# A transformer layer pair on one core: key and query turns placed between the chunks of the compressing products, and the products behind them inside the pair loop

## The chip, the cores and the metric

The kernel runs on one core of a Trainium2 chip. The core has five engines that run side by side and are tied together by semaphores: TensorE (PE in the profile; PEld are its weight loads), VectorE (DVE), ScalarE (ACT), GpSimd (POOL) and SyncE (SP, which issues DMAs). PE writes only to PSUM, whose banks are shared out by hand here; DVE and ACT copy from there to SBUF. The metric is the device time of one execution in microseconds (us), as the median of several runs.

## What is computed

Two blocks on 512 tokens of width 1024 follow each other; only a part of the second matters here, an attention over compressed keys and values, over blocks and over a window. Cut to that part:

```python
def compress(kv_raw, pos, w1, w2):
    blocks = kv_raw[:, idx] + pos            # 31 blocks of 32 tokens, step 16, 2 groups of 64 columns
    return jax.nn.gelu(blocks @ w1) @ w2     # hidden width 256, out 64

q  = rms_norm_2(q, q_norm_g)
kc = rms_norm_2(compress(kcr, ...), k_cmp_norm_g)
vc = compress(vcr, ...)
# for each block of queries
s = einsum('bqghd,bngd->bghqn', q, kc) * scale;  p = masked_softmax(s);  o_cmp = p @ vc
s = einsum(q_rope, k_slc_rope);                  o_slc = masked_softmax(s) @ v_slc
s = einsum(q_rope, k_win_rope);                  o_win = masked_softmax(s) @ v_win
out = g0 * o_cmp + g1 * o_slc + g2 * o_win

y = gelu(s5(u));  ssm = y * sigmoid(y @ glu_w + glu_b) * silu(z_s)
x + gate * (concat(out * silu(z_a), ssm) @ w_out)
```

## The kernel before

Every engine has its own program in one file, in the order in which it is written; no scheduler moves anything. A wait stands in front of the instruction that needs it, and all that is queued behind it on that engine waits too. On ACT and DVE the helper `step` also waits for each instruction's own end.

The stretch in question begins when PE has finished the gate products of the state-space half (`glu`, four banks). Then, on PE:

- *Turns.* `turn(name, blocks, ready)` transposes four 128x128 blocks into one of the two turn banks `U`; `turn_bank()` waits until the bank's last user but one has been copied out. DVE copies with `take_turn`. There are four turns of roped keys (`k2`), four of normed queries (`q`, they go to tiles 14 to 17) and four of roped queries (`qr`, tiles 18 to 21).
- *Compressing products.* `compress("k")` and `compress("v")` sum 32 products 62x256 each, in four chunks of eight; each chunk's weights are a DMA of 1 MB into one of four ring slots. SP asks for a chunk when the chunk four places before it has been used (`used`). ACT drains each result through Gelu into `HROW` ("hidden k", "hidden v").
- *What follows.* The hidden rows are turned, DVE copies them to `HIDK` and `HIDV`, PE makes the second products with `w2_k` and `w2_v` into the three `gemm` banks `G`, and ACT copies the results to `KCRAW` ("have kc") and, in four pieces, to `VB` ("have vcmp").

DVE meanwhile finishes the gate of the state-space half ("zs gated"), copies the key turns, rotates the queries in four parts (`rope`), makes the four GLU products ("ssm out") and copies the query turns.

Then comes the pair loop: 32 steps, each for two heads of one block of 128 queries; the first 16 are of the block attention, the next 16 of the window attention, with 1, 2, 3 and 4 blocks of keys in turn, four steps each. In step p PE makes the scores of pair p (`pair_scores`, into one of two double banks `PAIR`), the sums of pair p-2 (`pair_sums`) and the turns of the probabilities of pair p-1 (`pair_turns`). DVE takes the maximum of pair p, copies the turns of pair p-1, and at odd p closes a group of four heads (`pair_finish`); ACT makes the exponents. The compressed attention is spread over the same steps: `compressed(p)` on DVE (norm of the compressed keys in steps 0 and 1, their turned copy in step 2, softmax in steps `CMP_AT` to `CMP_AT` + 6 with `CMP_AT` = 4), `compressed_scores` on PE at step 4 (32 rows, 64 wide), `compressed_turn` at 11 and 12, `compressed_sums` at 14, 15, 16 and 18. At step 7 DVE also makes the product with the attention gate (2048 wide). The double banks swap their roles at `CMP_AT`, since the compressed scores take one.

In the profile L822 are the turns, L1145 the compressing products, L685 the other products by `product`, L1224 and L1227 pair scores, L1236 pair turns, L1250 pair sums, L1186 the compressed scores; on DVE L1766 is `take_turn`, L1808 `tt`, L1814 `stt`, L2522 the pair maxima; on ACT L1311 is `drain`, L1664 the copies to `VB`, L1674 the exponents.

## Time and profile before

| | us |
|---|---|
| median of three runs (lowest, highest) | 1598.39 (1596.98, 1600.68) |
| the profiled execution, its own time | 1598.52 |
| its span, first to last instruction | 1596.7 |
| PE busy | 1441.1 (90%) |
| DVE busy | 948.9 (59%) |
| ACT busy | 513.2 (32%) |
| mean granted clock of TensorE | 0.943 of full |

Busy shares are means over stages with very different limits. A timeline row gives the start, the length of a run of like instructions, the line, the tile written and the tiles read, the count, and in brackets the idle time before it with what ended it. The granted clock is 1.00 at 2.4 GHz and 0.50 at 1.2 GHz. A 32-bit matmul shows as two rows, a turn of a block as one.

### The profile page before, as it was taken

What the parts mean: (1) busy time and instruction counts of PE and PEld (TensorE: products, weight loads), DVE (VectorE), ACT (ScalarE), POOL (GpSimd) and SP (SyncE); (2) the same over time, 40 slices, a digit from 0 to 9 for tenths busy, and PEclk for the clock granted to TensorE, in tenths of its full rate; (3) what the DMA queues carried; (4) which work ended last, traced back from release to release, by engine and by line L of the source; (5) the groups of instructions that cost most, each with busy time, mean ns of one, the idle gap of its engine ahead of it and who ended that gap; (6) DMA issues with size and microseconds to landing.
All of it is one profiled execution on the core that took longest, in us unless ns stands there. A gap on an engine that the chain in (4) does not pass through costs nothing.

```text
span 1596.7 us, 18675 instructions
## 1 busy us (share of the span) xinstructions
PE 1441.1 (90%) x7046; PEld 1098.3 (69%) x7046; DVE 948.9 (59%) x1596; ACT 513.2 (32%) x829; POOL 52.7 (3%) x43
## 2 busy tenths in 40 slices
PE   5998888896999776998999999999798999988998
PEld 4758788784566654886788888888477854566653
DVE  6259767666266768774545555533593748758830
ACT  5346332231232565133432433533213222123300
POOL 0000000000000440000000000000000002000000
PEclk9999999997989879999999999999898999979999
DMA  5212111122222121452144434132321222410001
GB/s 226 71 53 80 66 40 53 60 91 67 89 88 73 47 74 54 143 182 97 66 145 181 150 144 160 55 109 94 111 82 37 80 78 81 166 71 1 1 1 53
DMA packets 39881, 140.50 MB, mean 88 GB/s; under 512 B 13040, under 2 KB 17520, under 8 KB 27248
## 3 DMA queue, kind: packets, MB, share of 16 engines
q1 hardware_dynamic: 34608, 130.53, 23.5%
q10 hardware_dynamic: 5184, 8.78, 1.5%
q8 instruction: 56, 0.92, 0.2%
q14 instruction: 33, 0.27, 0.1%
HBM read 128.42 MB, written 8.39 MB: 86 GB/s over the span
## 4 chain that ended last, share of the span: by engine, by line
PE 53%; DVE 6%; ACT 1%; issue 1%; ACTq 0%; DVEq 0%
PE turn L700 22%; PE score L685 6%; PE score L700 5%; PE sum L685 4%; PE turn L685 3%; PE sum L700 2%; PE sum L1250 2%; PE sum L1145 1%; PE score L1224 1%; PE turn L1236 1%; DVE heads L1808 1%; DVE work L1808 1%; DVE tiles L1814 1%; PE score L1289 1%; DVE probs L1766 0%
## 5 line engine op out<-in xcount | busy, mean ns | idle before, releaser
L1808 DVE TENSOR_TENSOR ring_r<-ring,heads_r 128x1024 fp32r<-128x1024 f32 (+3 forms) x153 | 176.3, 1152 | 223.1 <-ACT heads_r L1342 187.6
L1342 ACT ACTIVATE heads_r<-ring 128x1024 fp32r<-128x1024 f32 (+3 forms) x153 | 153.4, 1002 | 240.6 <-DMA ring<-wstream 129.5
L700 PE MATMUL score<-h_sb_r,heads_r 128*128 128x512 f32 x376 | 151.6, 403 | 0.0
L700 PE MATMUL turn<-tiles_r,heads_r 128*128 128x512 f32 x336 | 132.1, 393 | 0.0
L700 PE MATMUL turn<-h_sb_r,heads_r 128*128 128x512 f32 x304 | 119.7, 394 | 8.1 <-DVE ring_r L1808 8.1
L700 PE MATMUL turn<-wide_r,heads_r 128*128 128x512 f32 x312 | 121.9, 391 | 0.0
L700 PE MATMUL turn<-wide_r,ring_r 128*128 128x512 f32 x312 | 121.6, 390 | 0.0
L700 PE MATMUL score<-x_sb_r,heads_r 128*128 128x512 f32 x256 | 110.2, 430 | 8.9 <-DVE ring_r L1808 6.5
L700 PE MATMUL score<-x_sb_r,ring_r 128*128 128x512 f32 x256 | 103.8, 406 | 0.0
L700 PEld LDWEIGHTS score<-h_sb_r,heads_r 128*128 128x128 f32 x376 | 73.9, 197 | 13.7 <-issue 0.2
L700 PEld LDWEIGHTS turn<-tiles_r,heads_r 128*128 128x128 f32 x336 | 64.1, 191 | 13.2
L700 PEld LDWEIGHTS turn<-h_sb_r,heads_r 128*128 128x128 f32 x304 | 57.9, 190 | 20.5 <-issue 8.4
L700 PE MATMUL sum<-h_sb_r,heads_r 128*128 128x512 f32 x168 | 67.7, 403 | 0.0
L700 PEld LDWEIGHTS score<-x_sb_r,heads_r 128*128 128x128 f32 x256 | 51.2, 200 | 23.6 <-issue 10.6
L700 PEld LDWEIGHTS turn<-wide_r,ring_r 128*128 128x128 f32 x312 | 58.8, 189 | 12.3
L700 PEld LDWEIGHTS turn<-wide_r,heads_r 128*128 128x128 f32 x312 | 58.8, 188 | 12.3
L700 PEld LDWEIGHTS score<-x_sb_r,ring_r 128*128 128x128 f32 x256 | 50.8, 198 | 11.5
L1674 ACT ACTIVATE tiles<-score,stat 128x128 f32<-128x128 f32 (+3 forms) x64 | 33.7, 527 | 71.9 <-issue 65.3
L685 PE MATMUL score<-h_sb,ring 128*128 128x512 f32 x128 | 55.8, 592 | 0.0
L2571 POOL TENSOR_TENSOR stat<-stat,cst 128x4 f32<-128x4 f32 (+4 forms) x7 | 16.1, 2295 | 1187.2 <-DVE stat L1811 810.5
L1311 ACT ACTIVATE tiles<-score 128x512 f32<-128x512 f32 x39 | 24.3, 622 | 93.2 <-PE score L685 41.9
L700 PE MATMUL turn<-h_sb_r,ring_r 128*128 128x512 f32 x128 | 50.5, 395 | 0.0
(399 smaller groups left out, 2965.6 us busy)
## 6 DMA issues: line engine op xcount, KB each, us to landing
ring<-wstream SPq DMA_DIRECT2D x95, 1024.0 KB, 4.9
ring<-wstream SPq DMA_DIRECT2D x16, 704.0 KB, 4.3
ring<-gated SPq DMA_DIRECT2D x6, 1024.0 KB, 7.1
gated<-tiles ACTq DMA_DIRECT2D x15, 256.0 KB, 2.0
gated<-probs ACTq DMA_DIRECT2D x9, 256.0 KB, 2.0
x_sb<-xT SPq DMA_DIRECT2D x4, 512.0 KB, 5.7
x_sb<-xT ACTq DMA_DIRECT2D x1, 2048.0 KB, 8.0
outT<-x_sb SPq DMA_DIRECT2D x1, 2048.0 KB, 6.3
```

What stands on the lines that cost most here:

```text
L685: mm = pe.matmul(out, l, r, start=(i == 0), stop=(i == len(pairs) - 1))
L700: return pe.matmul(out, a, w, **k) if moving else pe.matmul(out, w, a, **k)
L1145: mm = pe.matmul(b[0:2 * NCMP, 0:256], CB[kv][:, 8 * i + l, :], w[:, l, :], start=(i + l == 0), stop=(8 * i + l == 31))
L1224: pe.matmul(PAIR_OF(p)[:, e * T:e * T + cols], TL[r, 18 + j, n * P:(n + 1) * P], KT2[r, 2 * a_ + j // 2, 0:cols], start=True, stop=False)
L1236: mm = pe.transpose(b[:, j * P:(j + 1) * P], PROB(i)[:, j * P:(j + 1) * P], ident)
L1250: mm = pe.matmul(OUT[g][:, h % 4 * P:h % 4 * P + P], PROBT(i)[:, j * P:(j + 1) * P], R2[:, j, at_v:at_v + P], start=(j == 0), stop=(j == n))
L1289: mm = pe.matmul(S[e], w[:, e, k, :], TL[:, 6 + k, :], start=False, stop=(k == 3))
L1311: step(act.activation(out, b, func, bias=bias, scale=scale), name, gemm_done)
L1342: step(act.activation(head_piece(p), chunk(name)[:, c:c + cols], ACT.Identity), f"head {p}")
L1674: step(act.activation(PROB(i)[:, 0:cols], PAIR_OF(p)[:, i % 2 * T:i % 2 * T + cols], ACT.Exp, bias=stat[:, 8 + i % 4:9 + i % 4], scale=1.0 ...
L1808: step(dve.tensor_tensor(out, a, b, op), name)
L2571: step(pool.tensor_tensor(v, v, half.broadcast_to([P, n]), ALU.pow), f"rstd {name}")
```

## The change

On PE, `compress` becomes a generator that stops after each chunk. Two key chunks come first, then two key turns, a chunk, two key turns, a chunk, two query turns, a value chunk and so on; the last value chunk comes after the hidden turn of the key. The hidden turn of the value moves into step 0 of the pair loop, the second product of the key into step 1 and that of the value into step 2; both go to turn banks. DVE copies their results in place of ACT. What followed of the compressed attention moves by one step (`CMP_AT` 4 to 5, turns at 12 and 13, sums at 15, 16, 17, 19). DVE's copies and rotations are put into the matching order. Cut to its core:

```diff
...
-    CMP_AT = 4
+    CMP_AT = 5
...
                         mm = pe.matmul(b[0:2 * NCMP, 0:256], CB[kv][:, 8 * i + l, :], w[:, l, :], start=(i + l == 0), stop=(8 * i + l == 31))
                     mm.then_inc(cmp_used if i < 3 else gemm_full, 1)
                     up(cmp_used if i < 3 else gemm_full, f"used cmp_{kv}{i}")
+                    yield
+
+            def hidden_turn(kv):
+
+                turn(f"hidden {kv}", [(HROW(kv)[0:2 * NCMP, k * P:(k + 1) * P], 2 * NCMP, 64 * k) for k in range(2)],
+                     (gemm_done, at(f"hidden {kv}")))
 
 
...
+            compressing = itertools.chain(compress("k"), compress("v"))
+            run(compressing, 2)
             for i in range(4):
                 turn(f"k2 {i}", [(K2(i)[:, n, :], P, n * P) for n in range(NT)], (dve_step, at("k roped")))
-            compress("k")
+                if i % 2:
+                    run(compressing, 1)
             for j in range(4):
                 turn(f"q {j}", [(R2[:, n, j * P:(j + 1) * P], P, n * P) for n in range(NT)], (dve_step, at("q normed")))
-            compress("v")
+                if j % 2:
+                    run(compressing, 1)
             for j in range(4):
                 turn(f"qr {j}", [(QR[:, n, j * P:(j + 1) * P], P, n * P) for n in range(NT)], (dve_step, at("q roped")))
-            for kv in "kv":
-                turn(f"hidden {kv}", [(HROW(kv)[0:2 * NCMP, k * P:(k + 1) * P], 2 * NCMP, 64 * k) for k in range(2)],
-                     (gemm_done, at(f"hidden {kv}")))
-            for kv in "kv":
-                b = gemm_bank()
+                if j == 1:
+                    run(compressing, 1)
+            hidden_turn("k")
+            run(compressing)
+
+            def hidden_out(kv):
+
+                b = turn_bank()
                 pe.wait_ge(turn_done, at(f"hidden T {kv}"))
...
-                mm.then_inc(gemm_full, 1)
-                up(gemm_full)
+                mm.then_inc(turn_full, 1)
+                up(turn_full)
 
...
                 if p == 0:
-                    pe.wait_ge(turn_done, at("hidden T v"))
+                    pe.wait_ge(turn_done, at("qrT 3"))
                 elif p == 1:
-                    pe.wait_ge(gemm_done, at("have vcmp"))
+                    pe.wait_ge(gemm_done, at("hidden v"))
                 elif p == CMP_AT + 1:
                     pe.wait_ge(dve_step, at("cmp masked"))
...
                 if 1 <= p <= 32:
                     for i in (2 * p - 2, 2 * p - 1):
                         pair_turns(i)
-                if p == 2:
+                if p == 0:
+                    hidden_turn("v")
+                if p in (1, 2):
+                    hidden_out("kv"[p - 1])
+                if p == 3:
                     turn("kc", [(KC2[0:NCMP, g, :], NCMP, 32 * g) for g in range(2)], (dve_step, at("kc normed")))
-                if p in (11, 12):
-                    compressed_turn(p - 11)
-                if p in (14, 15, 16, 18):
-                    compressed_sums((14, 15, 16, 18).index(p))
+                if p in (12, 13):
+                    compressed_turn(p - 12)
+                if p in (15, 16, 17, 19):
+                    compressed_sums((15, 16, 17, 19).index(p))
...
-            drain(KCRAW[0:NCMP, :], "have kc", cols=P, rows_=NCMP)
-            k = drained[0]
-            drained[0] += 1
-            act.wait_ge(gemm_full, k + 1)
-            for z in range(4):
-                r = slice(32 * z, 32 * z + 32)
-                step(act.activation(VB[r, :].rearrange("p (g d) -> p g d", g=2)[:, :, 64 * z:64 * z + 64],
-                                    G[k % 3][r, 0:P].rearrange("p (g d) -> p g d", g=2), ACT.Identity),
-                     "have vcmp" if z == 3 else None, gemm_done if z == 3 else act_step)
...
-            for i in range(4):
-                take_turn("kT 3" if i == 3 else None, KT2[:, i, :])
...
                 rope(qv[:, :, 0:32], qv[:, :, 32:64], cb, sb_, ta, tb, qd[:, :, 0:32], qd[:, :, 32:64], name="q roped" if n == NT - 1 else None)
+                if n < 2:
+                    for i in range(2):
+                        take_turn(None, KT2[:, 2 * n + i, :])
+            for j in range(4):
+                take_turn(None, TL[:, 14 + j, :])
             for j in range(4):
                 dve.wait_ge(gemm_done, at(f"glu {j}"))
                 stt(TL[:, 2 + j, :].rearrange("p (m a) -> p a m", a=STEP), H[:, 4 + j, :].rearrange("p (a m) -> p a m", a=STEP), 1.0,
                     TL[:, 10 + j, :].rearrange("p (a m) -> p a m", a=STEP), ALU.add, ALU.mult, "ssm out" if j == 3 else None)
-            for j in range(4):
-                take_turn(None, TL[:, 14 + j, :])
+                if j % 2:
+                    for i in (j - 1, j):
+                        take_turn(f"qrT {i}", TL[:, 18 + i, :])
             for cleared in (VB, part(rows, 2176, 512), part(rows, 2944, 128)):
                 step(dve.memset(cleared, 0.0), "cleared" if cleared is VB else None)
-            for j in range(4):
-                take_turn(None, TL[:, 18 + j, :])
             take_turn("hidden T k", HIDK[:, :, 0:2 * NCMP], cols=P, view=lambda v: v.rearrange("p (k t) -> p k t", k=2)[:, :, 0:2 * NCMP])
-            m = turned[0]
-            turned[0] += 1
-            dve.wait_ge(turn_full, m + 1)
-            for g in range(2):
-                src = U[m % 2][:, 0:P].rearrange("p (k t) -> p k t", k=2)[:, :, g * NCMP:(g + 1) * NCMP]
-                step(dve.tensor_copy(HIDV[:, :, g, :].rearrange("p k (r n) -> p k r n", r=4)[:, :, :, 0:NCMP],
-                                     src.unsqueeze(2).broadcast_to([P, 2, 4, NCMP])),
-                     "hidden T v" if g else None, turn_done if g else dve_step)
...
                 if p == 0:
-                    dve.wait_ge(gemm_done, at("have vcmp"))
+                    m = turned[0]
+                    turned[0] += 1
+                    dve.wait_ge(turn_full, m + 1)
+                    for g in range(2):
+                        src = U[m % 2][:, 0:P].rearrange("p (k t) -> p k t", k=2)[:, :, g * NCMP:(g + 1) * NCMP]
+                        step(dve.tensor_copy(HIDV[:, :, g, :].rearrange("p k (r n) -> p k r n", r=4)[:, :, :, 0:NCMP],
+                                             src.unsqueeze(2).broadcast_to([P, 2, 4, NCMP])),
+                             "hidden T v" if g else None, turn_done if g else dve_step)
+                if p == 1:
+                    take_turn(None, KCRAW[0:NCMP, :], cols=P, rows_=NCMP)
...
                     ts(stat[:, 32:34], stat[:, 32:34], 1.0 / 64, EPS, ALU.mult, ALU.add, name="mean kc")
-                if p == 1:
+                if p == 2:
+                    m = turned[0]
+                    turned[0] += 1
+                    dve.wait_ge(turn_full, m + 1)
+                    for z in range(4):
+                        r = slice(32 * z, 32 * z + 32)
+                        step(dve.tensor_copy(VB[r, :].rearrange("p (g d) -> p g d", g=2)[:, :, 64 * z:64 * z + 64],
+                                             U[m % 2][r, 0:P].rearrange("p (g d) -> p g d", g=2)),
+                             None, turn_done if z == 3 else dve_step)
                     dve.wait_ge(pool_step, at("rstd kc"))
...
-                if p == 2:
+                if p == 3:
...
-                if p in (11, 12):
-                    take_turn(f"cmp probsT {p - 11}", CMP_T[:, (p - 11) * T:(p - 10) * T])
-                if p in (14, 15, 16, 18):
-                    m, n = turned[0], (14, 15, 16, 18).index(p)
+                if p in (12, 13):
+                    take_turn(f"cmp probsT {p - 12}", CMP_T[:, (p - 12) * T:(p - 11) * T])
+                if p in (15, 16, 17, 19):
+                    m, n = turned[0], (15, 16, 17, 19).index(p)
```

How the order changes at three places. PE from the gate products to the first pair scores, before (turns of keys, queries and roped queries are L822, 16 blocks for four turns; a row here is one matmul):
```order
L822 MATMUL turn<-cst,work 128x128 x16
L1145 MATMUL score<-ring,heads 62x256 x32
L822 MATMUL turn<-cst,wide 128x128 x16
L1145 MATMUL sum<-ring,heads 62x256 x32
L822 MATMUL turn<-cst,work 128x128 x16
L822 MATMUL turn<-cst,work 128x62 x4
L685 MATMUL score<-sml,rows 31x64 x4
L685 MATMUL score<-sml,rows 128x64 x4
L1224 MATMUL score<-rows,tiles 128x128 x2
L1227 MATMUL score<-causal_b,ident_b 128x128 x2
```

The same stretch of PE in the changed kernel, up to the last query turns:
```order
L1145 MATMUL score<-ring,heads 62x256 x16
L822 MATMUL turn<-cst,work 128x128 x8
L1145 MATMUL score<-ring,heads 62x256 x8
L822 MATMUL turn<-cst,work 128x128 x8
L1145 MATMUL score<-ring,heads 62x256 x8
L822 MATMUL turn<-cst,wide 128x128 x8
L1145 MATMUL sum<-ring,heads 62x256 x8
L822 MATMUL turn<-cst,wide 128x128 x8
L1145 MATMUL sum<-ring,heads 62x256 x8
L822 MATMUL turn<-cst,work 128x128 x8
L1145 MATMUL sum<-ring,heads 62x256 x8
L822 MATMUL turn<-cst,work 128x128 x8
```

Each pair of turns now has a chunk of eight products ahead of it and one behind; the hidden turn of the key and the last chunk follow.

PE in steps 1 and 2 of the pair loop, before:
```order
L1224 MATMUL score<-rows,tiles 128x128 x2
L1227 MATMUL score<-causal_b,ident_b 128x128 x2
L1236 MATMUL turn<-cst,tiles 128x128 x2
L1224 MATMUL score<-rows,tiles 128x128 x2
L1227 MATMUL score<-causal_b,ident_b 128x128 x2
L1250 MATMUL sum<-wide,probs 128x128 x2
L1236 MATMUL turn<-cst,tiles 128x128 x2
```

PE from the end of step 0 to the end of step 2 in the changed kernel:
```order
L822 MATMUL turn<-cst,work 128x62 x2
L1237 MATMUL score<-rows,tiles 128x128 x2
L1240 MATMUL score<-causal_b,ident_b 128x128 x2
L1249 MATMUL turn<-cst,tiles 128x128 x2
L685 MATMUL turn<-sml,rows 31x64 x4
L1237 MATMUL score<-rows,tiles 128x128 x2
L1240 MATMUL score<-causal_b,ident_b 128x128 x2
L1263 MATMUL sum<-wide,probs 128x128 x2
L1249 MATMUL turn<-cst,tiles 128x128 x2
L685 MATMUL turn<-sml,rows 128x64 x4
```

The value's hidden turn (62 wide) and the two second products (L685, from `w2` in `sml`) have come in from ahead of the loop.

DVE in the pair loop, before, from the maximum of pair 10 to the copy of the first compressed turn (`heads<-turn`; `heads<-heads,stat` is the last product of the compressed softmax):
```order
L2522 TENSOR_REDUCE stat<-score 128x2
L1766 COPY probsT<-turn 128x384 x2
L1808 TENSOR_TENSOR heads<-heads,stat 128x1024
L2522 TENSOR_REDUCE stat<-score 128x2
L1766 COPY probs<-turn 128x384 x2
L1766 COPY heads<-turn 128x512
```

DVE in the changed kernel, from the maximum of pair 11 to the same copy:
```order
L2541 TENSOR_REDUCE stat<-score 128x2
L1774 COPY probs<-turn 128x384 x2
L1816 TENSOR_TENSOR heads<-heads,stat 128x1024
L2511 RECIPROCAL stat<-stat 128x4
L1816 TENSOR_TENSOR stat<-stat,wide 128x4
L2516 TENSOR_TENSOR work<-sum,stat 128x256
L2541 TENSOR_REDUCE stat<-score 128x2
L1774 COPY probsT<-turn 128x384 x2
L1774 COPY heads<-turn 128x512
```

The last softmax product now stands in a step that also closes a group of heads, and pair 12's maximum and a copy stand between it and the turn's copy.

## Rows read from the trace of the kernel before

**Rows 1.** Windows: start:end, length, busy us (count) by engine, granted clock, DMA share, GB/s.
```profile
1362.05:1407.75 45.70, 40.45 (x197) 25.54 (x195) 28.39 (x53) 4.31 (x8) 0.00 (x0) 0.93 0.61 207
1366.00:1369.00 3.00, 3.00 (x9) 1.67 (x9) 2.34 (x7) 0.78 (x4) 0.00 (x0) 0.50 0.13 52
1410.10:1427.00 16.90, 15.69 (x72) 13.25 (x72) 7.01 (x20) 4.39 (x19) 0.69 (x1) 0.50 0.00 1
1440.90:1447.40 6.50, 5.99 (x24) 4.58 (x25) 5.95 (x10) 2.68 (x8) 0.00 (x0) 0.50 0.00 0
```

**Rows 2.** Timeline of PE: start, us, line, tile, count, idle before and releaser.
```profile
1362.04 1.04 PE L822 MATMUL turn<-cst,work 128*128 128x128 f32 x8
1365.05 1.84 PE L822 MATMUL turn<-cst,work 128*128 128x128 f32 x8 [1.98 <-DVE rows L1766]
1366.82 15.15 PE L1145 MATMUL score<-ring,heads 128*62 128x256 f32 x64
...
1384.62 1.38 PE L822 MATMUL turn<-cst,wide 128*128 128x128 f32 x8 [1.62 <-DVE tiles L1766]
1385.93 15.71 PE L1145 MATMUL sum<-ring,heads 128*62 128x256 f32 x64
...
1405.32 0.33 PE L822 MATMUL turn<-cst,work 62*128 62x62 f32 x2 [0.39 <-DVE tiles L1766]
1405.73 0.61 PE L685 MATMUL score<-sml,rows 128*31 128x64 f32 x8
1406.77 1.08 PE L685 MATMUL score<-sml,rows 128*128 128x64 f32 x8 [0.43 <-ACT work L1311]
1407.77 0.49 PE L1224 MATMUL score<-rows,tiles 64*128 64x128 f32 x4
...
1411.02 0.94 PE L1236 MATMUL turn<-cst,tiles 128*128 128x128 f32 x2 [1.15 <-ACT tiles L1674]
```

**Rows 3.** Timeline of PE's weight loads, in the value product.
```profile
1389.59 11.60 PEld L1145 LDWEIGHTS sum<-ring,heads 128*62 128x62 f32 x54 [0.20 <-issue]
```

**Rows 4.** Timeline of DVE, from the gate product to the query copies.
```profile
1361.98 2.29 DVE L1808 TENSOR_TENSOR tiles<-tiles 128x2048 f32<-128x2048 f32 x1
...
1368.37 0.89 DVE L1808 TENSOR_TENSOR wide<-wide,cst 128x256 f32<-128x256 f32 x2
...
1379.39 4.44 DVE L1814 SCALAR_TENSOR_TENSOR tiles<-h_sb,tiles 128x512 f32<-128x512 f32 x4
1383.87 2.93 DVE L1766 COPY tiles<-turn 128x512 f32<-128x512 f32 x4
```

**Rows 5.** Timeline of ACT, at the start of the pair loop.
```profile
1407.94 1.17 ACT L1664 ACTIVATE tiles<-score 32x128 f32<-32x128 f32 x4 [1.24 <-PE score L685]
1409.12 1.28 ACT L1674 ACT_TABLE_LOAD   x1
1410.42 0.37 ACT L1674 ACTIVATE tiles<-score,stat 128x128 f32<-128x128 f32 x1
```

**Rows 6.** Timeline of PE in the pair loop.
```profile
1417.31 6.93 PE L1186 MATMUL score<-rows,tiles 128*128 128x64 f32 x32
1424.16 1.23 PE L1224 MATMUL score<-rows,tiles 64*128 64x256 f32 x4
...
1427.03 0.75 PE L1224 MATMUL score<-rows,tiles 64*128 64x256 f32 x4
...
1441.41 2.08 PE L1250 MATMUL sum<-wide,probsT 128*128 128x128 f32 x8 [2.38 <-DVE probsT L1766]
...
1453.48 0.66 PE L1196 MATMUL turn<-cst,heads 128*128 128x128 f32 x4 [1.12 <-DVE probs L1766]
```

**Rows 7.** Timeline of DVE in the pair loop: gate product, last softmax product.
```profile
1437.61 2.29 DVE L1814 SCALAR_TENSOR_TENSOR tiles<-h_sb,tiles 128x2048 f32<-128x2048 f32 x1
...
1450.62 1.22 DVE L1808 TENSOR_TENSOR heads<-heads,stat 128x1024 f32<-128x1024 f32 x1
```

**Rows 8.** The page's DMA part: loads of weight chunks, KB each, us to landing.
```profile
ring<-wstream SPq DMA_DIRECT2D x95, 1024.0 KB, 4.9
```

More of the change, by code:

```diff
@@ L1244, in pair_sums @@
                     if i < 8:
-                        pe.wait_ge(*((y_done, 4) if i == 0 else (gemm_done, at("have vcmp"))))
+                        pe.wait_ge(*((y_done, 4) if i == 0 else (gemm_done, at("hidden v"))))
                     else:
```

## The prediction, made before the changed kernel was run

> **What bounds the kernel now.** I read four views, in this order: the timeline of TensorE (PE) from the gate products to the pair loop, the windows with the granted clock, then the timelines of VectorE (DVE) and ScalarE (ACT) over the same stretch. Of 1596.7 us the change touches 1362 to about 1460. In its first part, 1362.04 to 1407.77, PE ends nearly every wait: the chain of waits is made of its products. But 45.73 us pass there for far less work. PE stands still 1.98 us before the third key turn and 1.62 us before the third query turn, both times until DVE frees one of two turn banks [rows 2]; DVE is then still at the 2.29 us products of the state-space gate or at the four 1.11 us GLU products [rows 4]. After each pause the clock falls: 1366 to 1369 was granted 0.50, which is 1.2 GHz [rows 1]. So the two compressing products take 15.15 and 15.71 us [rows 2], where at full clock a row takes 0.215 us (11.60 us for 54) [rows 3], or 13.75 us for 64. Then a chain without cover follows: hidden turn, second products, ACT's copies of their results (four in 1.17 us), a wait of PE for them, the first scores, and the exponent's table (1.28 us) [rows 2, 5].
>
> In the loop's first steps PE waits for ACT again, the clock goes to 1.2 GHz at 1410 and stays there to 1427 [rows 1]; the compressed scores run in 6.93 us, 0.217 us a row [rows 6]. From pair 5 on (1427.03) the clock is back, and DVE is the engine that is late, up to about pair 11: PE waits 2.38 us for it at 1441.41 and 1.12 us at 1453.48 [rows 6]. After the first of these the clock is down once more, 1440.9 to 1447.4 [rows 1].
>
> **Part 1, turns between chunks: 11.3 us less.** In the new order PE needs for this stage:
> - 128 rows of the compressing products by 0.2148 us [rows 3]: 27.5;
> - twelve turns, two by two at 1.04 us [rows 2]: 6.2;
> - one hidden turn, 0.33 [rows 2], and about 0.3 until a turn bank is free for it (the copy before it takes 0.73, a turn 0.52): 0.6.
>
> That is 34.4 us from 1362.04, so the first scores at 1396.4 instead of 1407.77. What goes: waits of 2.0 and 1.6 us, the low clock's 3.4 us (15.15 + 15.71 - 27.5), 2.5 us from the second hidden turn at 1405.32 to the scores, and small waits between turns. I take the clock at its full level for the whole stage, since nothing in it pauses PE for more than 0.3 us.
>
> The cover is DVE. Its copies (0.73 each), four rotations (2.76 each, 1368.37 to 1379.39) and GLU products [rows 4] must end before PE comes back to a bank. The tightest place is the third query turn: PE reaches it at 1382.4; DVE ends the gate product at 1364.3, has 0.6 us of small copies, waits for the first key turn until 1369.6, and then does four copies and three rotations, to about 1381.0, and the first query copy to 1381.8. So 0.6 us are left, and 1 us of lateness there would cost about 0.4. ACT's part (both drains) ends long before it is wanted. The loads: the fourth key chunk is asked for when the gate products leave their slot, at 1362, and lands 4.9 us later [rows 8], at 1367; PE wants it at 1374.5. Each value chunk is asked for when the key chunk four before it is used, and is wanted 8 us later or more. These cost nothing; SP passes no new wait.
>
> **Part 2, second products and copies inside the loop: 3.2 us back.** The value's hidden turn and both second products now stand in steps 0 to 2. At full clock they are 0.3 + 0.61 + 1.08 = 2.0 us [rows 2]; at half clock, at 0.217 us a row where weights are 128 wide, 0.5 + 1.2 + 1.7 = 3.4. Bounds: nothing, if they fill PE's wait for the first exponent (about 1.2 us before 1411.02, [rows 2]), and 3.4 plus 1.2, if DVE queues behind them: in step 2 it waits for the value product with the maximum of pair 3 behind it, and ACT's exponents behind that. I take 3.2, near the upper end, because the hidden turn comes ahead of that wait and the products behind it. ACT loses five copies (four of them 1.17 us, [rows 5]); DVE gets them, in steps in which it waits for PE anyway. So from the first scores to those of pair 5 it takes 19.3 + 3.2 = 22.5 us: pair 5 at 1419 instead of 1427.03, 8.1 us ahead.
>
> The first exponents still wait for the table. The row shows the load at 1409.12 for 1.28 us and the exponent at 1410.42, 0.02 us after its end [rows 5]; I cost it at that. The Trainium skill ("ScalarE: Activation LUTs", What ACT_TABLE_LOAD costs) counts a drain of about 1.38 us with each switch, 2.66 us together; the trace does not show it here, and by it the sum would be 1595 (an estimate).
>
> **Part 3, pair 5 at half clock: 1.4 us back.** The low clock ended at 1427 behind the compressed scores and pair 4's wider products. In the new order one sparse step more precedes those scores, and pair 5 follows them. A step took 2.87 us at half clock (1424.16 to 1427.03, [rows 6]); at full clock half of that. Zero, if the clock comes back earlier.
>
> **Part 4, the compressed softmax one step later: 1.7 us back.** Its DVE steps move from 4, 5, 6, 8, 9, 10 to 5, 6, 7, 9, 10, 11. Steps of odd number also end a group of heads. Step 7 now holds the subtraction (1.22), that end and the 2.29 us product with the attention gate [rows 7], so the wait of 2.38 us becomes about 3.4. What step 6 no longer holds gives most of that back. In step 11 the last product (1.22, [rows 7]) stands ahead of a group's end and of pair 12's maximum, and PE's first compressed turn waits for the bank behind them: 1.12 becomes about 2.4. Net 0.4 + 1.3. Bounds 0 and 4.7 (below). Later steps are the same but for one sum on DVE.
>
> **Sum.** 11.3 - 3.2 - 1.4 - 1.7 = 5.0 us. The profiled execution took 1598.5 us (span 1596.7, 1.8 around it); 1598.5 - 5.0 = **1593.5**. That execution is 0.1 us above the median of the three times, so I leave it.
>
> **Rivals.**
> *A third fall of the clock.* If PE's wait before the first compressed turn grows to 2.4 us, it is as long as those at 1363 and 1439, after which the clock fell. The price is that of the fall at 1440.9: 5.99 us busy in 6.5 at half clock, 3.0 us. Against it: at 1453.48, after 1.12 us, it stayed. 1593.5 + 3.0 = 1596.5.
> *The clock comes back before the compressed scores.* Pair 4's wider products now stand ahead of them. Then they take 3.5 us, and part 3 is nothing: 4.9 us better, of which DVE, late from pair 5 on, takes back some 1.7: 1590.3. Against it: the level stayed low through steps 2 and 3 before.
> *The low clock goes on behind pair 5.* From pair 5 to 1441.41 lie 14.4 us with 2.4 of waiting [rows 6], so up to 12 us of PE's work; at half clock that is 24: up to 9.6 us more, 1603; from some 8 us of it on the kernel is slower. Against it: the clock returned after one dense stretch at 1427 and again at 1447. The low level is sure in the first steps, not beyond.
> *The switch of tables stalls* for as long again as the load (1.28 us, [rows 5]) now that it follows the Gelu with nothing between: 1594.8. Against it: 0.02 us in the row.
>
> **How the numbers follow.** Forecast 0.44 (alone 1592 to 1596), third fall 0.27, early clock 0.20, lasting low clock 0.06, table 0.03. The likeliest gives 1593.5. For 8 in 10 the range takes in most of the third fall and half of the early clock: 1589.8 to 1597.6. A measurement of this kernel can tell about 0.2%, 3.2 us: below 1595.2 lie 0.82 of the forecast (0.36), the early clock (0.20), and 0.04 of the others, so faster 0.60; slower is the lasting low clock, 0.06; the rest, 0.34, is the same.
>
> **What would show it.** Right: PE without a wait over 0.5 us from the gate products to the first scores, clock at 2.4 GHz there, 34 to 35 us long; pair 5's scores 22 to 23 us after the first pair's. Wrong in part 1: a wait before the third query turn. In part 2: pair 3's maximum over 1 us behind its scores. In part 4: PE waits of over 2.4 us in steps 9 and 12, and the clock after each.

## The result and the profile after

The changed kernel took 1588.68 us (median of five; 1584.48 to 1590.87) beside 1598.39: ratio 0.9938, 95% interval 0.9925 to 0.9951. Six further executions in a later measurement had a median of 1590.13, ratio 0.9946 (0.9931 to 0.9962). So it is faster by 8.6 to 9.9 us, where the forecast was 4.9. The lower end of its range was 1589.8: the first median lies below it, the second just inside. The sign was right and the size was not: the change gained nearly twice as much.

The profiled execution has a span of 1586.8 us, 9.9 less than before. The windows of its stretches, which answer [rows 1] (start:end, length, busy us and count of PE, PEld, DVE, ACT, POOL, granted clock, DMA share, GB/s):

```profile
1362.20:1397.70 35.50, 35.08 (x179) 22.03 (x178) 27.52 (x51) 3.67 (x6) 0.00 (x0) 1.00 0.69 237
1398.50:1410.00 11.50, 7.18 (x60) 5.16 (x61) 8.06 (x28) 4.95 (x17) 0.70 (x1) 1.00 0.26 91
1410.60:1420.50 9.90, 9.90 (x48) 9.12 (x46) 3.14 (x5) 1.69 (x6) 0.00 (x0) 0.50 0.01 2
1434.20:1437.20 3.00, 3.00 (x13) 1.59 (x12) 2.55 (x5) 1.34 (x4) 0.00 (x0) 0.50 0.02 5
```

From the gate products to the first scores PE now stands still for 0.4 us out of 35.5, at 2.4 GHz throughout. Behind them it is busy for only 7.18 us out of 11.50, still at 2.4 GHz; the clock falls after that, to 1.2 GHz for 9.9 us, and once more for 3.0. Before, it was low for 16.9 and 6.5 us there.

PE's timeline, which answers [rows 2] and [rows 6] (start, us, line, operation, tile written and tiles read, count, idle time before with its releaser):

```profile
1358.67 3.60 PE L685 MATMUL score<-tiles,ring 128*128 128x512 f32 x8
1362.20 7.12 PE L1145 MATMUL score<-ring,heads 128*62 128x256 f32 x32
1369.25 1.09 PE L822 MATMUL turn<-cst,work 128*128 128x128 f32 x8
1370.27 3.67 PE L1145 MATMUL score<-ring,heads 128*62 128x256 f32 x16
1373.87 1.09 PE L822 MATMUL turn<-cst,work 128*128 128x128 f32 x8
...
1393.86 0.33 PE L822 MATMUL turn<-cst,work 62*128 62x62 f32 x2 [0.42 <-DVE tiles L1774]
...
1397.72 0.49 PE L1237 MATMUL score<-rows,tiles 64*128 64x128 f32 x4
...
1400.94 0.30 PE L1249 MATMUL turn<-cst,tiles 128*128 128x128 f32 x1 [1.74 <-ACT tiles L1682]
...
1408.76 0.30 PE L822 MATMUL turn<-cst,rows 31*128 31x31 f32 x2 [1.40 <-DVE probs L1774]
...
1410.67 6.93 PE L1199 MATMUL score<-rows,tiles 128*128 128x64 f32 x32
1417.53 1.23 PE L1237 MATMUL score<-rows,tiles 64*128 64x256 f32 x4
...
1420.69 0.70 PE L1237 MATMUL score<-rows,tiles 64*128 64x256 f32 x4
...
1432.84 1.17 PE L1263 MATMUL sum<-wide,probsT 128*128 128x128 f32 x8 [3.64 <-DVE probsT L1774]
...
1448.60 0.66 PE L1209 MATMUL turn<-cst,heads 128*128 128x128 f32 x4 [2.25 <-DVE probsT L1774]
1449.19 1.13 PE L1237 MATMUL score<-rows,tiles 64*128 64x512 f32 x4
...
1530.79 7.13 PE L1306 MATMUL score<-tiles,ring 128*128 128x512 f32 x16 [0.85 <-DVE tiles L2528]
```

Chunks and turns follow each other without a gap (1369.25, 1370.27, 1373.87 and so on); 1397.72 are the scores of the first pair, 1417.53 those of pair 5, 1420.69 those of pair 6, 1449.19 those of pair 13, and 1530.79 is the first output product behind the loop. The same places in the kernel before, as far as they are not among the rows ahead of the prediction:

```profile
1358.60 3.60 PE L685 MATMUL score<-tiles,ring 128*128 128x512 f32 x8
...
1428.86 0.70 PE L1224 MATMUL score<-rows,tiles 64*128 64x256 f32 x4
...
1458.47 1.13 PE L1224 MATMUL score<-rows,tiles 64*128 64x512 f32 x4
...
1539.01 8.83 PE L1289 MATMUL score<-tiles,ring 128*128 128x512 f32 x16 [0.85 <-DVE tiles L2509]
```

With the rows at 1407.77 and 1427.03 [rows 2, 6] they split the 9.9 us of the span:

| stretch | before, us | after, us | difference | prediction |
|---|---|---|---|---|
| start of the last gate product | 1358.60 | 1358.67 | +0.07 | 0 |
| to the first scores | 49.17 | 39.05 | -10.12 | -11.3 |
| to pair 5 | 19.26 | 19.81 | +0.55 | +3.2 |
| to pair 6 | 1.83 | 3.16 | +1.33 | +1.4 |
| to pair 13 | 29.61 | 28.50 | -1.11 | +1.7 |
| to the product behind the loop | 80.54 | 81.60 | +1.06 | 0 |
| to the end of the span | 57.69 | 56.01 | -1.68 | 0 |

The last line is no part of the change. The product at 1539.01 took 8.83 us, with a mean granted clock of 0.66 from 1539 to 1544; after, the same product took 7.13. A second profile of the kernel before (b2, below) shows it at 7.13 too. Without it the two traces differ by 8.2 us, which is nearer to the second of the two ratios.

### The profile page after: what moved, and what is told of

Same layout as the page of the kernel before. It is cut to its first block, busy times and chain, and to the rows that moved or that the text cites. A ratio compares the mean times of both kernels' runs of the same rounds, so it can differ in the third digit from the quotient of the medians.

```text
span 1586.8 us, 18674 instructions
## 1 busy us (share of the span) xinstructions
PE 1432.6 (90%) x7046; PEld 1092.9 (69%) x7046; DVE 950.3 (60%) x1601; ACT 511.9 (32%) x824; POOL 52.7 (3%) x43
## 3 DMA queue, kind: packets, MB, share of 16 engines
q10 hardware_dynamic: 5184, 8.78, 1.5%
## 4 chain that ended last, share of the span: by engine, by line
PE 54%; DVE 4%; ACT 1%; issue 1%; ACTq 0%; DVEq 0%
PE turn L700 22%; PE score L685 7%; PE score L700 5%; PE sum L685 4%; PE turn L685 3%; PE sum L700 2%; PE sum L1263 2%; PE sum L1145 1%; PE score L1145 1%; PE score L1237 1%; PE turn L1249 1%; PE turn L822 1%; DVE stat L2541 1%; PE turn L1118 1%; DVE probs L1774 0%
## 5 line engine op out<-in xcount | busy, mean ns | idle before, releaser
L685 PE MATMUL score<-h_sb,ring 128*128 128x512 f32 x128 | 55.8, 592 | 0.0
```

Of the source, the lines that this page charges most:

```text
L685: mm = pe.matmul(out, l, r, start=(i == 0), stop=(i == len(pairs) - 1))
```

## The experiments

### The parts one by one

The turns alone (e1), with DVE's copies in the matching order and all else as in the kernel before:

```diff
+            compressing = itertools.chain(compress("k"), compress("v"))
+            run(compressing, 2)
...
+            hidden_turn("k")
+            run(compressing)
+            hidden_turn("v")
             for kv in "kv":
                 b = gemm_bank()
...
```

> The kernel before with the turns set between the chunks of the compressing products, and nothing else: the hidden turn of the value, both second products and ACT's copies still stand ahead of the pair loop. Theory A: interleaving carries the whole gain and the loop's share only costs; then the first scores come about 10 us earlier than 1407.77 and the time is 1588 or less. Theory B: a good third of the 10 us is the chain of hidden turn, second products and copies behind the last value chunk, which is still bare here (0.4 drain, 0.3 turn, 0.9 copies, 1.1 product, waits between); then the first scores come at about 1401 (7 us earlier) and the time is 1591 to 1592. In both, steps 4 to 12 of the loop look as they did before: waits of some 2.4 and 1.1 us.

Measured: 1593.04 us beside 1598.9, ratio 0.9959 (0.9946 to 0.9972), so some 6 us faster (5.9 by the medians, 6.6 by the ratio). Theory B holds for the place of the first scores; the time is 1 us above its range. PE's timeline:

```profile
1398.98 0.30 PE L822 MATMUL turn<-cst,work 62*128 62x62 f32 x2 [0.62 <-ACT work L1323]
...
1400.40 1.08 PE L685 MATMUL score<-sml,rows 128*128 128x64 f32 x8 [0.55 <-DVE rows L2441]
1401.41 0.49 PE L1236 MATMUL score<-rows,tiles 64*128 64x128 f32 x4
```

The first scores stand 42.16 us behind the start of the last gate product, 7.0 less than before. The hidden turn of the value still waits 0.62 us for the Gelu and its second product 0.55 us for DVE's copies. The other 3.1 us of the stretch come only when this chain leaves it. Of the two waits that were to stay as they were, that of 2.38 us stands again at step 9; in place of the 1.12 us before the first compressed turn PE waits 1.74 us two rows earlier, with a fall of the clock behind it.

The other half alone (e2), second products and softmax as in the changed kernel, turns as before:

```diff
-            compressing = itertools.chain(compress("k"), compress("v"))
-            run(compressing, 2)
...
+            run(compress("k"))
...
+            run(compress("v"))
```

> The changed kernel with the turns back behind whole compressing products: only the second products, their copies and the compressed softmax are moved. Theory A (the loop's share costs, as the prediction had it): 1598.4 less some 2.5 us for the bare chain ahead of the loop, plus 3.2 + 1.4 + 1.7, about 1602. Theory B (the loop's share costs 0.55 from the first scores to pair 5's, 1.3 at pair 5, and nothing by the softmax one step later): about 1597.5, and 1596 if the softmax one step later gains 1.6.

Measured: 1598.8 us beside 1598.9, ratio 1.0006 (0.9991 to 1.0022). Alone it makes no difference that is clear of the noise. It lies between the theories, nearer to B: the first scores come 46.65 us behind the last gate product, 2.5 less, as both said; but the way from them to pair 5 takes 22.24 us in its profile instead of 19.26, which is the cost of the prediction's part 2. Its profiled execution is one of the longer of twelve (1604.2; they run from 1594.4 to 1604.4), in which the clock fell some 4 us behind the first scores:

```profile
1409.93 0.49 PE L1230 MATMUL score<-rows,tiles 64*128 64x128 f32 x4 [0.39 <-DVE tiles L1767]
...
1432.17 1.23 PE L1230 MATMUL score<-rows,tiles 64*128 64x256 f32 x4
```

### The same two kernels again

> The kernel before once more, for a second profile. Theory A: the low clock at the first 16 rows behind the loop (8.83 us instead of 7.13) belongs to the kernel and stands here too, near 1539. Theory B: where the clock falls there differs from execution to execution; here the 16 rows may take 7.1 us. The low stretch from 1410 to 1427 and that behind 1440 should stand again, if they follow from PE's waits.

> The changed kernel once more, for a second profile. Theory A: the clock stays up until the compressed scores (fall at 1410) and behind the loop (16 rows in 7.1 us) in this execution too. Theory B: both are chance and one of them differs here; the time then moves by 1.7 us for the rows behind the loop, by 2 to 4 us for a fall at 1400.

Kernel before (b2): 1602.94 us. The low clock stands again at the loop's start, now from 1411, two us ahead of the first scores (1412.98), to 1435, and once more behind the wait for DVE in step 9. But it does not stand behind the loop, where the output product takes 7.13 us. So theory B holds for the place behind the loop: the fall there came in one execution of this kernel and not in the other.

Changed kernel (a2): 1597.59 us, 8.9 us more than its first profile, with the same program. Its windows, the first scores being at 1400.55:

```profile
1365.03:1400.50 35.47, 35.06 (x179) 22.04 (x178) 25.85 (x51) 3.67 (x6) 0.00 (x0) 1.00 0.68 237
1401.00:1404.00 3.00, 1.27 (x13) 0.76 (x11) 1.68 (x4) 2.18 (x6) 0.00 (x0) 1.00 0.77 251
1404.60:1428.30 23.70, 22.77 (x108) 18.77 (x109) 11.58 (x35) 4.57 (x19) 0.70 (x1) 0.50 0.01 3
```

Pair 5's scores and the first compressed turn:

```profile
1423.14 1.23 PE L1237 MATMUL score<-rows,tiles 64*128 64x256 f32 x4
...
1455.99 1.12 PE L1209 MATMUL turn<-cst,heads 128*128 128x128 f32 x4 [2.25 <-DVE probsT L1774]
```

The interleaved stretch has the same length and is busy for the same 35.06 us. But here the clock fell between 1404.0 and 1404.6, some 4 us behind the first scores, and stayed low for 23.7 us; in the first profile it fell some 12.5 us behind them, for 9.9 us. In the 3.0 us before the early fall PE had been busy for 1.27. Pair 5 comes 22.59 us behind the first scores: the prediction's 22.5, to a tenth. It also shows the third fall that was named as a rival, at the first compressed turn (1455.99), behind a wait of 2.25 us. Only 2.8 us of the 8.9 lie between the first scores and pair 5. Another 2.8 lie ahead of the changed part (the last gate product starts at 1361.51, and the clock is low for some 10 us more ahead of it), 2.2 between pair 5 and pair 13, and 1.1 from there to the product behind the loop.

> The changed kernel again, timed beside the three variants of it. Theory A: the first profile (clock falls 12 us behind the first scores, for 10 us) is what most executions do: median about 1588.7, few above 1594. Theory B: executions are split between that and the second profile (clock falls 3.5 us behind the first scores, for 24 us; 1597.6): the median comes out between, at 1590 to 1594, and the spread is as wide as that of the kernel before.

Measured (a3): 1590.13 us median, six executions from 1587.85 to 1597.35. Of all twelve executions of the changed kernel ten lie between 1584.5 and 1591.1, and two at 1597.4 and 1597.6. Its new profile repeats the first one (fall some 12 us behind the first scores, pair 5 after 19.83 us). The median lies 1.4 us above that of theory A, at the edge of B's range, but the times do not fall into two like halves. Theory A is the nearer: the profiles of e4 and e5, whose programs are the same up to the compressed scores or just ahead of them, have the late fall too, so it stands in four of five. That the two long executions fell early is not shown, since a time can grow by low clock elsewhere.

### Holding the clock

Nine products of no use, 128x256 each, on the changed kernel (e3), placed where PE waits in steps 1 to 3:

```diff
+            def hold(count):
+
+                for _ in range(count):
+                    pe.matmul(OUT[1][:, 0:256], ident, R2[:, 0, 0:256], start=True, stop=True)
...
+                if p == 1:
+                    hold(4)
...
+                if p == 2:
+                    hold(2)
...
+                if p == 3:
+                    hold(3)
```

> The changed kernel with nine idle products (128x256, into a sum bank that is not in use yet) on TensorE where it waits in steps 1, 2 and 3 of the pair loop. Theory A (the low clock behind 1398 comes from TensorE's waits there and is what makes executions differ): the clock stays at 2.4 GHz through the compressed scores, they take 3.5 us instead of 6.93, pair 5 comes 15 to 17 us behind the first scores instead of 19.8 to 22.6, and the median falls by 4 to 6 us. Theory B (the clock falls for other reasons, or VectorE and ScalarE set these steps anyway): scores at half clock as before, median the same or up to 1.5 us longer for the added rows.

Measured: 1585.52 us median, four executions between 1584.60 and 1586.21, ratio to the kernel before 0.9913 (0.9900 to 0.9926). On the same chip the changed kernel took 1590.13. The product behind the loop starts 168.78 us after the last gate product, 3.3 less than in the changed kernel. Theory A holds: the window from the first scores to pair 5, and the compressed scores in it:

```profile
1398.55:1414.90 16.35, 15.89 (x121) 12.75 (x120) 9.80 (x32) 6.46 (x22) 0.69 (x1) 1.00 0.18 66
```

```profile
1399.87 1.95 PE L1271 MATMUL sum<-wide,cst 128*128 128x256 f32 x8
...
1411.29 3.68 PE L1199 MATMUL score<-rows,tiles 128*128 128x64 f32 x32
1414.90 0.70 PE L1237 MATMUL score<-rows,tiles 64*128 64x256 f32 x4
...
1429.31 2.08 PE L1263 MATMUL sum<-wide,probsT 128*128 128x128 f32 x8 [3.64 <-DVE probsT L1784]
```

PE is busy for 15.89 us of 16.35 and keeps 2.4 GHz; the scores take 3.68 us instead of 6.93. Pairs 1 to 4 stand where they stood without the idle rows, to 0.02 us: those ran wholly inside waits. What falls away is the fall at the compressed scores. In step 9 the clock still falls, now during the wait of 3.64 us for VectorE, and stays low for some 7 us, where the changed kernel has 3.

The same on the kernel before (e8), with sixteen idle products from the hidden turns to step 3 (the expectation below says fourteen; the trace has 32 rows of them, two to a product):

> The kernel before with fourteen idle products on TensorE, from the hidden turns to step 3 of the loop. Theory A (there, too, the low clock from 1410 to 1427 comes from TensorE's waits, and costs what the changed kernel gains in its first steps): no low clock up to pair 5, the compressed scores take 3.5 us, 14 to 15.5 us from the first scores to those of pair 5 instead of 19.3, some 0.5 to 1 us more ahead of the loop, and a median 3 to 4 us below that of the kernel before. Theory B (the clock falls there for another reason): no change, or 1 us more.

Measured: 1593.63 us beside 1599.41, ratio 0.9964 (0.9951 to 0.9978). Added work alone makes the kernel before 5.8 us faster. Its trace shows 3.6 of them up to the product behind the loop (176.78 us from the last gate product instead of 180.41), as theory A had it, and 1.7 in that last stretch, where the product takes 7.13 us here; that the remainder is spread is not shown.

```profile
1408.93:1423.70 14.77, 14.77 (x109) 12.27 (x108) 7.54 (x24) 6.03 (x21) 0.70 (x1) 1.00 0.00 1
```

From the first scores to pair 5 it takes 14.86 us instead of 19.26, at 2.4 GHz. So the low clock there cost the kernel before at least 4.4 us; 0.8 of them are spent again on the added rows ahead of the loop. With the clock held there on both sides the change is worth 0.9913 / 0.9964 = 0.995, some 8 us, and 8.0 us in the traces up to the product behind the loop (176.78 - 168.78): the gain is not a gift of the clock behind the first scores. Ahead of them it is in part, since the low stretches behind the pauses in the turns went with those pauses (granted clock 0.93 before [rows 1], 1.00 after).

### VectorE's work behind pair 5

The product with the attention gate in step 5, where DVE stands idle (e4):

```diff
                 if p == CMP_AT:
+                    dve.wait_ge(act_step, at("tanh za"))
+                    za4 = tiles[:, 6 * T:10 * T]
+                    stt(za4, h_sb[:, 0:4 * T], 1.0, za4, ALU.add, ALU.mult)
                     dve.wait_ge(score_full, at("full cmp"))
...
-                if p == 7:
-                    dve.wait_ge(act_step, at("tanh za"))
...
```

> The changed kernel with VectorE's 2.29 us product with the attention gate moved from step 7 to the start of step 5, where VectorE stands 5.81 us waiting for the compressed scores. Theory A (the prediction's part 4: VectorE's work in steps 7 to 9 sets the end there): TensorE's wait of 3.64 us at step 9 becomes about 1.3, the clock does not fall behind it, and the time falls by 2.3 to 4 us. Theory B (what is gained at step 9 is waited for again at step 12, since VectorE is late on the whole from step 6 on): the wait at step 12 grows from 2.25 and the time falls by less than 1 us.

Measured: 1587.12 us beside 1590.13 for the changed kernel, ratio to the kernel before 0.9934 (0.9915 to 0.9953); four of the six executions took 1585.3 to 1587.9, two 1593.5 and 1595.0. The times alone do not part the two kernels, their intervals overlap; the trace does. Theory A:

```profile
1416.89 1.23 PE L1237 MATMUL score<-rows,tiles 64*128 64x256 f32 x4
...
1429.88 1.17 PE L1263 MATMUL sum<-wide,probsT 128*128 128x128 f32 x8 [1.31 <-DVE probsT L1774]
...
1445.25 0.66 PE L1209 MATMUL turn<-cst,heads 128*128 128x128 f32 x4 [2.25 <-DVE probsT L1774]
```

The wait at step 9 is 1.31 us, the clock does not fall there, and the wait at step 12 is 2.25 as it was. From pair 5 to pair 13 it takes 28.95 us instead of 31.66, 2.7 less: the 2.29 us of the product and, since the clock does not fall, a little more. The product behind the loop starts 169.33 us after the last gate product, 2.8 less.

The softmax put back (e5) to where the kernel before has it, all else as in the changed kernel:

```diff
-    CMP_AT = 5
+    CMP_AT = 4
...
-                if p in (12, 13):
+                if p in (11, 12):
...
-                if p in (15, 16, 17, 19):
+                if p in (14, 15, 16, 18):
```

> The changed kernel with the compressed scores, their softmax, turns and sums one step earlier, where the kernel before has them; interleaving and second products in the loop stay. Theory A (the prediction: the shift costs 1.4 at pair 5 and 1.7 by the meeting with the ends of head groups): about 3 us less than the changed kernel. Theory B (the shift costs 1.06 us, seen from pair 13 to the end of the loop, and nothing before): about 1 us less. Theory C: the turned compressed keys are not there at step 4, TensorE waits 0.5 to 1 us for them, and the time is the same.

Measured: 1589.25 us beside 1590.13, ratio to the kernel before 0.9938 (0.9925 to 0.9951): no difference from the changed kernel. Theory A, the prediction's, falls; C holds:

```profile
1410.29 6.69 PE L1199 MATMUL score<-rows,tiles 128*128 128x64 f32 x32 [0.64 <-DVE rows L2481]
...
1434.33 1.81 PE L1263 MATMUL sum<-wide,probsT 128*128 128x128 f32 x8 [2.39 <-DVE probsT L1774]
...
1446.19 0.66 PE L1209 MATMUL turn<-cst,heads 128*128 128x128 f32 x4 [1.17 <-DVE probs L1774]
```

PE waits 0.64 us for the turned keys, and the waits behind are 2.39 and 1.17, where the changed kernel has 3.64 and 2.25. Yet the product behind the loop starts 172.08 us after the last gate product, in the changed kernel 172.12. The windows from pair 5 to pair 13 tell why. Kernel before, changed kernel, softmax put back, gate product early:

```profile
1427.03:1458.47 31.44, 25.94 (x169) 18.88 (x168) 28.43 (x48) 11.79 (x36) 0.00 (x0) 0.89 0.00 1
```

```profile
1417.53:1449.19 31.66, 25.10 (x165) 18.08 (x165) 28.39 (x46) 10.93 (x32) 0.00 (x0) 0.90 0.00 1
```

```profile
1419.77:1451.17 31.40, 25.20 (x169) 18.16 (x168) 28.43 (x48) 12.13 (x36) 0.00 (x0) 0.93 0.00 1
```

```profile
1416.89:1445.84 28.95, 23.76 (x166) 17.25 (x165) 26.09 (x45) 10.95 (x32) 0.00 (x0) 0.95 0.00 1
```

DVE's column is 28.4 us in the first three, and the lengths are 31.4, 31.7 and 31.4, although the softmax lies in other steps and PE waits at other places. In the fourth it is 26.1 and the length 28.95. Where the order changes and the sum does not, the length stays; where the sum falls, the length falls with it. The sum is not all of it: with as much work of DVE, 28.4 us, the second profiles took 31.95 (b2) and 33.90 (a2), e1 32.6 and e2 32.5, with mean granted clocks of 0.91, 0.85, 0.89 and 0.85. How much of that is the clock was not worked out.

### Both together, and more

The idle products of e3 and the early product of e4 in one kernel (e6):

> The changed kernel with both edits: the nine idle products in steps 1 to 3 and VectorE's product with the attention gate at the start of step 5. Theory A (the two act in different stretches, the clock up to step 5 and VectorE's work behind it): their gains in the traces, 3.3 and 2.8 us, add up; the loop ends about 6 us earlier than the changed kernel's and the median is 1582 to 1584. Theory B (with the clock held, VectorE reaches step 5 without the 5.8 us of waiting that hid the product): 1585 or more.

Measured: 1581.82 us (five executions, 1581.44 to 1585.64) beside 1599.41, ratio 0.9894 (0.9876 to 0.9912). It is the lowest median of all, some 7 us below the changed kernel.

```profile
1427.06 1.17 PE L1263 MATMUL sum<-wide,probsT 128*128 128x128 f32 x8 [1.31 <-DVE probsT L1784]
...
1524.60 7.13 PE L1316 MATMUL score<-tiles,ring 128*128 128x512 f32 x16 [0.85 <-DVE tiles L2538]
```

The product behind the loop starts 165.01 us after the last gate product, 7.1 less than in the changed kernel, against 3.3 and 2.8 from the two apart, so theory A holds and the two together give 1 us more than their sum. From 1265 to the end of PE's work the clock is not low anywhere in this profile, so the fall in step 9, which e3 still had, is gone too.

Two more moves on top of that, in the same sense (e7), with the last softmax product, the turns and the sums of the compressed attention a step later too:

```diff
-                if p in (1, 2):
-                    hidden_out("kv"[p - 1])
+                if p == 1:
+                    hidden_out("k")
...
+                    hidden_out("v")
-                if p in (12, 13):
-                    compressed_turn(p - 12)
+                if p in (13, 14):
+                    compressed_turn(p - 13)
```

> The kernel of e6_fill_za with two further moves: the value's second product and its four copies on VectorE go behind the turn of the compressed keys in step 3, and the last softmax product, the compressed turns and sums come one step later still. Theory A (VectorE's sum of work between pair 5 and pair 13 sets that stretch): 1.2 to 1.9 us of it leave the stretch, the wait at the first compressed turn falls from some 2 us, and the time is 1 to 2 us below that of e6_fill_za. Theory B (as from the kernel before to the changed one, the later sums give it back in steps 16 to 20): the same time.

Measured: 1582.40 us, ratio 0.9898 (0.9882 to 0.9915): the same. From pair 5 to pair 13 it does take 2.3 us less (25.72, DVE 24.07), but the compressed sums now come in steps in which DVE has little to spare:

```profile
1465.72 1.13 PE L1218 MATMUL turn<-tiles,heads 128*128 128x256 f32 x4 [1.14 <-DVE probsT L1785]
...
1471.28 1.13 PE L1218 MATMUL turn<-tiles,heads 128*128 128x256 f32 x4 [1.50 <-DVE probsT L1785]
...
1522.87 8.78 PE L1317 MATMUL score<-tiles,ring 128*128 128x512 f32 x16 [0.86 <-DVE tiles L2539]
```

Waits of 1.14 and 1.50 us stand where e6 has 0.37 and 0.30, the loop ends 0.8 us earlier than in e6, and in this execution the clock fell behind it (8.78 us for 16 rows). Theory B, for the most part.

## Why the prediction was wrong, step by step

The steps that failed are two: the price of part 2, taken at a clock that was called sure, and the waits of parts 3 and 4, priced one by one. Up to the product behind the loop the forecast was 5.0 us less and the traces show 8.2. The 3.3 us between them are 2.65 of part 2 and 2.9 of parts 3 and 4, less 1.2 that part 1 fell short and 1.06 that the sum left out.

**Part 1, 11.3 us less: right, 10.1.** The stage is 35.5 us long and without a wait over 0.42, at 2.4 GHz, and the third query turn found its bank free. The 1.2 us that are missing lie in one term: I took a row of the products at 0.2148 us from a long run [rows 3]. In chunks of 16 with turns between, the next turn starts 3.60 us behind a chunk's start (1370.27 to 1373.87), 0.225 a row, and the first 32 rows take 7.05 (1362.20 to 1369.25). Together that is 28.65 us for 128 rows, 1.15 more than the 27.5 of the sum.

**Part 2, 3.2 us back: wrong in the usual execution, 0.55.** The term was mis-sized by one sentence of it, that the low level is sure in the first steps. With the clock low from some 4 us behind the first scores the step is right (22.59 us to pair 5 in the second profile, 22.24 in e2). But in two of three profiles, and, as far as times can tell, in some ten of twelve executions, the clock fell only with the compressed scores, some 12 us behind the first scores, so hidden turn and second products ran at 2.4 GHz. With the clock held in both kernels the part costs 16.35 - 14.86 = 1.5 us (added rows stand in both), and in the usual execution the shorter low clock (3.5 us of cost against 4.4) takes 0.9 of that back. The fall stands near the first scores in both profiles of the kernel before (2.3 us behind them, and 1.9 ahead) and 2 us behind them in e1. So a second profile of that kernel would have shown only that the place moves. What failed was to carry the place over to a kernel with another order ahead of it; why the fall comes late there most of the time stays open.

The sign that I had named against this part did come, though the part was cheap:

```profile
1405.72 1.25 DVE L2467 COPY tiles<-turn 32x128 f32<-32x128 f32 x4 [0.94 <-PE turn L685]
...
1407.95 0.42 DVE L2541 TENSOR_REDUCE stat<-score 128x2 f32<-128x256 f32 x1
```

Pair 3's maximum starts 1.7 us behind the end of its scores (1406.25), since DVE waits for the value's second product and copies it first. PE then stands 1.40 us before the turn at 1408.76. So the queueing behind DVE was read rightly, and the rows at half clock were not. None of the rivals held what came, a clock that stays up to the compressed scores and falls there; the early return that I gave 0.20 would have had nearly its time, 1590.3, by another way.

**Part 3, 1.4 us back: there, and worth nothing.** Pair 5 to pair 6 took 3.16 us instead of 1.83. But behind it PE waits for DVE anyhow, and what pair 5 loses is that much less of waiting later: from pair 5 to pair 13 it took 31.44 us before and 31.66 after, 0.22 more, where parts 3 and 4 had counted 3.1.

**Part 4, 1.7 us back: the waits were right, their sum was not.** The prediction had 3.4 and 2.4 us for the waits in steps 9 and 12; they are 3.64 and 2.25. It charged 0.4 and 1.3 us for them, the growth of the waits less what earlier steps were to give back. The stretch is set by the sum of DVE's work, which the change leaves at 28.4 us, so that a wait that grows in one step shrinks in the others. e5 agrees: at the loop's end parts 3 and 4 together are worth 0.0 where I counted 3.1, or at most 0.7 if e5's own wait of 0.64 us for the turned keys is set aside. The step that failed is the sum over single waits in a stretch that one engine fills to nine tenths.

**What the sum left out.** The compressed sums a step later cost 1.06 us behind pair 13, which I had at nothing. Against e5 the changed kernel loses 1.42 us there and has gained 1.39 up to pair 13. 1.68 us of the difference of the two profiles lie behind the loop, where the clock fell in the first profile of the kernel before and not in its second; I count them to no part of the change.

**The rivals.** The third fall came in one of three profiles of the changed kernel. The low clock did not last behind pair 5: it was back 3 us behind its scores, and some 5 us behind them in the second profile. The table did not stall:

```profile
1397.88 0.38 ACT L1328 ACTIVATE work<-sum 62x256 f32<-62x256 f32 x1 [18.85 <-PE sum L1145]
1399.04 1.28 ACT L1682 ACT_TABLE_LOAD   x1 [0.78 <-DVE stat L2541]
1400.34 0.37 ACT L1682 ACTIVATE tiles<-score,stat 128x128 f32<-128x128 f32 x1
```

The load takes 1.28 us and is ACT's next instruction behind the Gelu. It starts 0.78 us after the Gelu's end, when the first maximum is there, and the exponent follows 0.02 us after its end. The drain of 1.38 us that the Trainium skill counts ("ScalarE: Activation LUTs", What ACT_TABLE_LOAD costs) is not in the trace here either.

## What to carry to other kernels

Where one engine is busy for nine tenths of a stretch, price an edit there by what it adds to or takes from that engine's sum, and not by the waits that it makes or removes step by step. A sparse stretch of TensorE cost twice here, once by its waits and once by the low clock that follows: products with no use, put into waits that are there anyway, gave 4.6 us in the changed kernel and 5.8 in the kernel before, by the medians. Before a clock level is carried over into the sum of a changed order, take a second profile to see whether its place moves, and price the case in which the clock stays up.

## What the runs showed of the hardware

The place at which TensorE's clock falls is not fixed by the program. In three profiles of the changed kernel it fell some 12, 12 and 4 us behind the first scores, with PE's rows up to the early fall alike to 0.01 us. The Trainium skill ("TensorE: Matmul & The Clock Gate", Part 1: The HAM clock gate) says that the gate's clockwork does not start anew with a kernel, and that the same kernel therefore changes level at another place from run to run. The traces agree that the place moves; why it does they do not show. They show the price: executions of the changed kernel took 1584.5 us at a mean granted clock of 0.951, 1588.7 at 0.949, 1590.9 at 0.945 and 1597.6 at 0.940, and the two profiles of the kernel before 1598.5 at 0.943 and 1602.9 at 0.939. Where the waits at the loop's start are filled the times lie closer: four executions of e3 within 1.6 us, beside six of the changed kernel within 9.5 and six of e4, which leaves those waits, within 9.7. The other kernels with filled waits lie between: e8 within 3.5 us (six), e6 within 4.2 and e7 within 4.7 (five each). Four or five are few; that the early fall never comes with the waits filled is not shown.

A fall does not need a long wait: the 23.7 us at 1.2 GHz in the second profile came behind waits of at most 1.73 us. I had not expected that work without use makes a kernel faster by about half as much as a change like this one.
